# Six stages in the low-rank pass, and an earlier place for the gate product, in a four-layer streaming encoder

## The reference

```python
z = h @ w_in
cq, ckv, kr, bq, bk, bv, gate = jnp.split(z, [o1, o2, o3, o4, o5, o6], axis=-1)
q = (rmsnorm(cq, g_q) @ w_uq).reshape(bsz, s_len, A_HEADS, A_NOPE + A_ROPE)
q = jnp.concatenate([q[..., :A_NOPE], rope(q[..., A_NOPE:], pos)], axis=-1)
kv = (rmsnorm(ckv, g_kv) @ w_ukv).reshape(bsz, s_len, A_HEADS, A_NOPE + A_VDIM)
kr = rope(kr[:, :, None, :], pos)
k = jnp.concatenate([kv[..., :A_NOPE], jnp.broadcast_to(kr, ...)], axis=-1)
oa = chunk_causal_attention(q, k, kv[..., A_NOPE:])
ob = chunk_band_attention(bq, bk, bv, rel_table)
y = jnp.concatenate([oa, ob], axis=-1) * jax.nn.silu(gate)
return y @ w_out
```

## Time and profile before

| What | us |
|---|---|
| Median of 3 runs | 4638.97 |
| Lowest and highest run | 4635.57, 4826.6 |
| Profiled execution | 4641.6 |
| Its span on the slowest core (core 2) | 4640.0 |
| Spans of the other cores | 4610.8 to 4636.3 |
| TensorE busy with matmuls | 4253.2 |
| VectorE busy | 1785.6 |
| ScalarE busy | 1186.5 |
| GpSimd busy | 457.9 |

### The profile page before, as it was taken

The page is one execution under the profiler, slowest core; times in us unless marked ns, Lnnn a source line. Parts: engine busy times, 40 slices in busy tenths (PEclk is TensorE's granted clock), DMA queues, the critical chain, the costliest instruction groups (busy, mean ns, idle before and its releaser), DMA issues.

```text
span 4640.0 us, 80438 instructions; the slowest of 8 cores (4610.8 to 4640.0 us)
## 1 busy us (share of the span) xinstructions
PE 4253.2 (92%) x30381; PEld 2427.0 (52%) x30884; DVE 1785.6 (38%) x3721; ACT 1186.5 (26%) x2187; POOL 457.9 (10%) x482
## 2 busy tenths in 40 slices
PE   0378889999999899999999799999999999999998
PEld 0145667667744345444444566677774444544444
DVE  0563442333357326111465444233335743611133
ACT  1123443222232123000222344322223222300011
POOL 1020110000000001222002101000000000122200
PEclk9999999999999999999999999999999999999999
DMA  9877775454396787457767566555339665623543
GB/s 198 158 140 109 115 106 73 61 67 49 56 225 191 159 172 202 76 91 106 200 191 119 84 92 83 66 65 76 44 47 221 191 155 146 155 37 41 89 161 136
DMA packets 666891, 550.93 MB, mean 119 GB/s; under 512 B 416352, under 2 KB 602976, under 8 KB 647568
## 3 DMA queue, kind: packets, MB, share of 16 engines
q0 software_dynamic: 321760, 239.09, 36.8%
q1 hardware_dynamic: 344752, 306.65, 24.0%
HBM read 620.54 MB, written 100.76 MB: 155 GB/s over the span
## 4 chain that ended last, share of the span: by engine, by line
PE 83%; DMA 6%; DVE 4%; issue 3%; another core or an unknown queue 2%; SPq 1%; ACT 1%; POOL 0%; DVEq 0%; ACTq 0%; POOLq 0%
PE PS L300 79%; PE PS L298 4%; DMA RG<-R 2%; DMA W<-sg_w_in 1%; SPq L337 1%; DMA RG<-w_mod 1%; DVE R L322 1%; DVE R L325 1%; DVE RG L319 1%; DMA RG<-ab_w_out 1%; DMA VR<-R 1%; DMA R<-tb 0%; ACT R L310 0%; POOL R L322 0%
## 5 line engine op out<-in xcount | busy, mean ns | idle before, releaser
L300 PE MATMUL PS<-RG,W 128*128 128x512 bf16 x6370 | 1479.7, 380 | 73.0 <-DVE RG L319 26.3
L300 PE MATMUL PS<-W,RG 128*128 128x128 bf16 (+3 forms) x13887 | 1491.4, 261 | 53.4 <-DVE R L325 24.5
L310 ACT ACTIVATE R<-PS 128x512 bf16<-128x512 f32 (+5 forms) x1536 | 777.4, 515 | 2368.9 <-PE PS L300 1591.5
L300 PEld LDWEIGHTS PS<-W,RG 128*128 128x128 bf16 x13952 | 1045.6, 98 | 531.6 <-issue 81.5
L300 PEld LDWEIGHTS PS<-RG,W 128*128 128x128 bf16 x6528 | 631.5, 98 | 797.3 <-issue 103.5
L300 PE MATMUL PS<-RG 128*128 128x512 bf16 (+3 forms) x3896 | 952.2, 374 | 19.4 <-DMA RG<-ab_w_out 3.9
L300 PEld LDWEIGHTS PS<-RG 128*128 128x128 bf16 x3968 | 388.4, 98 | 397.6 <-issue 13.7
L325 DVE CAST R<-PS 128x512 bf16<-128x512 f32 (+1 forms) x352 | 233.6, 667 | 491.3 <-PE PS L300 406.1
L310 ACT ACTIVATE RG<-PS 128x2048 bf16<-128x2048 f32 (+2 forms) x128 | 151.6, 1184 | 878.5 <-PE PS L300 868.1
L322 DVE TENSOR_TENSOR RG<-PS,R 128x512 bf16<-128x512 f32 x128 | 88.5, 692 | 705.0 <-PE PS L300 703.6
L300 PE MATMUL PS<-R 128*128 128x128 bf16 (+3 forms) x1411 | 319.8, 283 | 4.8 <-DVE R L319 2.4
(11 more groups left out here) (79 smaller groups left out, 1955.6 us busy)
## 6 DMA issues: line engine op xcount, KB each, us to landing
W<-w_mod POOLq DMA_DIRECT2D x64, 1024.0 KB, 10.1
RG<-w_mod POOLq DMA_DIRECT2D x32, 1024.0 KB, 16.0
W<-ab_w_in POOLq DMA_DIRECT2D x64, 512.0 KB, 8.0
VR<-R SPq DMA_DIRECT2D x128, 256.0 KB, 3.5
R<-VR SPq DMA_DIRECT2D x32, 1024.0 KB, 5.4
W<-sg_w_in POOLq DMA_DIRECT2D x32, 1024.0 KB, 13.5
XB<-R SPq DMA_DIRECT2D x20, 1024.0 KB, 6.5
RG<-XB SPq DMA_DIRECT2D x20, 1024.0 KB, 5.7
```

Of the source, the lines that this page charges most:

```text
L300: P.op("pe", lambda e: e.matmul(o, lhsT, rhs, start=start, stop=stop), r=r, w=w, sig=sig)
L310: P.op("act", lambda e: e.activation(out=o, in_=i, func=func, **kw), r=r, w=w, wp=wp)
```

## The change

The list of stages gets two more entries, blocks 8 and 10, and the tiles go round six stages in place of four; each of the six gets its memset. The countdown of the gate product becomes 3 in place of 6.

```diff
-            SG = (12, 14, 20, 22)
+            SG = (12, 14, 20, 22, 8, 10)
 
             def stage(t):
-                a = SG[t % 4]
+                a = SG[t % 6]
                 return Rb(a, 2), RT(a, 2)
 
-            for t in range(4):
+            for t in range(6):
                 sv, svt = stage(t)
                 mset("dve", sv[:, 832:960], 0.0, w=svt)
...
                     act(th, bank(b), AF.Tanh, r=[PS_t[b]], w=tht, scale=0.5)
-                    later.append([6, b, lambda: stt("dve", Y[:, yc[n], tgs(tg)], th, 1.0, bank(b), ALU.add, ALU.mult, r=[PS_t[b]] + tht,
+                    later.append([3, b, lambda: stt("dve", Y[:, yc[n], tgs(tg)], th, 1.0, bank(b), ALU.add, ALU.mult, r=[PS_t[b]] + tht,
```

## The result

The changed kernel took 4599.28 us in the median, the kernel before 4639.68 beside it: a ratio of 0.9915, with a 95% interval of 0.9893 to 0.9938. That is 40 us or 0.85% less, within the 2% that count as the same, and inside the range; 4592 was forecast. The profiled execution took 4598.65 us, 43.0 less than the one before. Its slowest core is core 3 and not core 2, so starts of the two traces are not compared, only distances. Averaged over the eight cores of each profiled execution, the span fell from 4626.2 to 4579.7 us, by 46.5.

What follows compares the result with a forecast made beforehand. TensorE was taken as the bound, busy 4253.2 of 4640.0 us. Stages 8.0 plus product 38.7 make 46.7 us off 4641.6, so 4594.9; the median lies 2.6 below: 4592, range 4580 to 4618.

Steps and rivals of the forecast that it cites:

- The stages: Low-rank passes of layers 0 and 2: one of four stage-write stalls goes in each, 4.2 and 3.8 us, sum 8.0.
- The shared token: Stages 20 and 22 both hold token V5, so a write waits 3.83 us for its neighbour's transpose, even at first use.
- rival one: Six stages end every stall in the low-rank passes, 19 us less in place of 8: 4581; chance 0.06.
- What comes next: After the low-rank pass, TensorE's 8.46 us wait for the last transpose, 16.09 us long with weight loads behind it, stays.
- The product: Gate product moved ahead of the next evacuation: 28 waits of 1.54 us removed, 43.1, less 4.4 given back: 38.7 us.
- A: Behind each head's second gate group, before a q group: 1.54 us wait goes, 0.40 comes in 11 of 14 cases.
- B: Behind each head's third gate group: the product already waits for its tanh, so 0.24 us stays.
- C: Behind the last gate group, before a k of two matmuls: 1.54 us goes; a modulation product may move in, no change.
- Two: At C the wait only changes its name, against a margin of 0.2 us: 4599 to 4614; chance 0.15.
- Three: VectorE's earlier products hold up masks or bias additions; outweighs the gain once 0.47 us is lost per product; chance 0.03.
- Four: The edits do nothing, because a product is also emitted when its bank is next taken: 4639; chance 0.02.

## Why the prediction was right

**The stages.** Right in mechanism and size. One stall of four went in each pass: 37.33 - 33.22 = 4.1 us in pass 1 (4.2 forecast) and, from 2531.34 to 2568.39 before and 2512.68 to 2545.95 after, 3.8 us in pass 2 (3.8 forecast; tile 3 in the kernel before, then tiles 3 and 15 in the changed one, and the earlier trace rows for the fourth):

```profile
2531.34 0.48 DVE L319 SCALAR_TENSOR_TENSOR R<-PS,st,W 128x256 bf16<-128x256 f32 x1 [4.78 <-DMA RG<-R]
```

```profile
2512.68 0.48 DVE L319 SCALAR_TENSOR_TENSOR R<-PS,st,W 128x256 bf16<-128x256 f32 x1 [4.05 <-DMA RG<-R]
...
2545.95 0.48 DVE L319 SCALAR_TENSOR_TENSOR R<-PS,st,W 128x256 bf16<-128x256 f32 x1 [3.87 <-DMA RG<-R]
```

TensorE's waits behind the passes fell a little less, by 3.7 and 3.4 us to 6.23 and 5.79, where 5.7 and 5.3 were forecast. The shared token was argued from a stall at the first use of a stage; the run with four separate stages shows it. The Trainium skill says that a repeating gap can mean too few buffers (Perfetto Trace Analysis, Optimization Strategy), which stood beside rival one. Here it did not mean that: six stages kept the gap of 3.8 us, four had none.

**What comes next.** The wait for the last transpose stayed, as forecast, at 8.2 us in layer 2 and 10.2 in layer 0. Its cause, only argued there, is now shown.

**The product.** All 28 waits of 1.54 us went, and 0.40 came in at A behind modulation products. B kept its 0.24. The sum was 38.7; the two stretches of heads became 15.8 + 19.8 = 35.6 us shorter. In layer 2, 14 x 1.54 less 5 x 0.40 is 19.6, and 19.8 was measured. In layer 0, with 6 x 0.40, it would be 19.2, and 3.4 us are missing.

**The term that was mis-sized** is the sentence on C: that a due modulation product may come before the second k group and "the 0.40 behind it moves along, no change". The order of instructions shows that it does move there, and the 0.40 moves along. But one such move put a step that waits for a DMA ahead of two evacuations, and TensorE lost 3.21 us on this core. I had counted that product's matmuls, addition and load, and not the DMA for which its last step waits. With the place kept, the wait was 0.32 us on the slowest core, but three others had 1.25 to 2.20, so the move is only a part of it. On three cores of the changed kernel the wait is at most 0.3 us, and the mean gain of layer 0 is 18.5 us, 0.7 below the 19.2.

**The sum.** 7.9 + 35.6 = 43.5 lies close to the 43.0 between the two profiled executions, but that is luck, since the two are different cores. The pass of layer 0 begins on TensorE at 285.66 before and at 278.34 after, 7.3 us that neither edit touches. From there to the first matmul behind the last transpose it is 77.61 us before and 77.43 after: 0.2 us less, not 4.1. VectorE's first write of the pass before, then TensorE's start of the pass and that write after:

```profile
296.17 0.48 DVE L319 SCALAR_TENSOR_TENSOR R<-PS,st,W 128x256 bf16<-128x256 f32 x1
```

```profile
278.34 12.31 PE L300 MATMUL PS<-W,RG 128*128 128x320 bf16 x80
...
290.74 0.47 DVE L319 SCALAR_TENSOR_TENSOR R<-PS,st,W 128x256 bf16<-128x256 f32 x1
```

VectorE waits for the rope tables before it, so it came 12.40 us behind TensorE's start in place of 10.51, 1.9 us later, and the last transpose took 2.0 us longer. The means of the eight cores are the better test. The passes became 4.3 and 4.3 us shorter, the stretches of heads 18.5 and 20.6, the rest 1.2 longer: 46.5, beside the sum of 46.7. The slowest core, which is what is timed, gained less, 43.0 in these executions and 40.4 in the medians: the cores of the changed kernel lie further apart (34 us from the shortest span to the longest, 29 before).

**The rivals.** One fell with the stalls that remain. Two fell: the margin of 0.2 us at C held at 13 of 14 places (the one wait for line 319 there, 0.28 us, is at the last k group of head 5 in layer 2), and so it is on all eight cores. Three has a mechanism that exists, but only once the product is emitted at once, and then for 3.6 us in all, while 47 would be needed. Four fell.

**Open** stays the time of the moved modulation product and of the product at once: 3 us is below what the few runs could tell, so these two rest on the trace alone. Open is also why the g_post DMA lands later on some cores.

## What to carry to other kernels

When a stall repeats every n-th tile, look at its first occurrence: if the buffer had never been used, more buffers are no cure; look for what two neighbours share. Where TensorE alternates between two PSUM banks, let VectorE empty the older bank first: an evacuation that is emitted ahead of an earlier bank's last reader costs TensorE both (1.54 us at each of 28 places here). And when an emission slot opens earlier, list every wait of what may move into it, DMAs above all, for VectorE runs in order and others' evacuations stand behind.

## What was not expected of the hardware

A DMA transpose of one 128 x 1024 tile took 2.7 us within the pass, and 16.1 and 18.1 us (kernel before and changed kernel, layer 0) when three loads of 2.5 MB in all were issued just behind it. Holding those loads back until it had landed, 4 us, gave back 18 us of TensorE's waits in the two layers, and no wait for these weights came in.
